# Splitting a unit's top-16 search and numbering between batches of dot products

## What is computed

```python
def peer(h, w_query, sub_keys, u_table, v_table):
    q = (x @ w_query).reshape(-1, PEER_HEADS, 2, KEY_DIM)
    s = jnp.einsum('nhid,hikd->nhik', q, sub_keys)
    top_s, top_i = lax.top_k(s, PEER_TOPK)
    cand_s = (top_s[..., 0, :, None] + top_s[..., 1, None, :])
    cand_i = (top_i[..., 0, :, None] * N_KEYS + top_i[..., 1, None, :])
    best_s, pos = lax.top_k(cand_s, PEER_TOPK)
    idx = jnp.take_along_axis(cand_i, pos, axis=-1)
    g = jax.nn.softmax(best_s, axis=-1)
    act = gelu(einsum('nd,nhkd->nhk', x, u_table[idx])) * g
    return einsum('nhk,nhkd->nd', act, v_table[idx])
```

## Time and profile before

| | before |
|---|---|
| median of 3 runs | 1032.12 us (1031.52 to 1033.51) |
| profiled execution | 1032.95 us, its span 1031.1 us |
| PE busy | 822.1 us (80%) |
| DVE busy | 669.9 us (65%) |
| ACT busy | 245.9 us (24%) |
| POOL busy | 420.1 us (41%) |
| gathers (queue q0) | 36864 packets, 268.45 MB |

### The profile page before, as it was taken

How to read it: one execution, slowest core, us unless ns; L and a number is a source line. 1 busy time by engine, 2 the same in 40 slices (tenths; PEclk the granted TensorE clock), 3 DMA queues, 4 the chain that set the end, 5 groups by cost and what they waited for, 6 DMA issues and landing times. The chain is left out here.

```text
span 1031.1 us, 9412 instructions
## 1 busy us (share of the span) xinstructions
PE 822.1 (80%) x2733; PEld 412.4 (40%) x2733; DVE 669.9 (65%) x1409; ACT 245.9 (24%) x764; POOL 420.1 (41%) x379
## 2 busy tenths in 40 slices
PE   5799867799888988779768787876777886877875
PEld 1276523346448964323323333332333332333332
DVE  7669999971337753477478568569579559645443
ACT  1421102125211123122222223132222213122120
POOL 1026756730001116455544453544543553644430
PEclk9999989999899999898998998998988998998898
DMA  9911126445033728999999999999999999999991
GB/s 360 401 32 64 75 89 237 176 174 215 0 123 139 291 82 332 422 422 421 422 421 422 422 422 421 421 421 422 421 421 421 422 422 420 421 421 422 421 401 48
DMA packets 43782, 322.54 MB, mean 313 GB/s; under 512 B 5768, under 2 KB 6600, under 8 KB 7520
## 3 DMA queue, kind: packets, MB, share of 16 engines
q0 software_dynamic: 36864, 268.45, 62.8%
q1 hardware_dynamic: 6512, 53.47, 13.3%
q10 hardware_dynamic: 368, 0.18, 0.1%
HBM read 320.86 MB, written 1.23 MB: 312 GB/s over the span
## 5 line engine op out<-in xcount | busy, mean ns | idle before, releaser
L737 PE MATMUL psum<-ring,arena 128*128 128x512 f32 x672 | 329.6, 649 | 90.3 <-ACT arena L982 90.2
L1437 DVE CUSTOM_DVE_ANT_0 ring<-ring,h 128x1024 f32<-128x1024 f32 x168 | 202.7, 1225 | 161.6 <-DMA ring<-uv_table,arena 160.6
L1093 POOL DMA_INDIRECT ring<-uv_table,arena x168 | 201.5, 1199 | 252.6 <-PE psum L737 187.0
L737 PEld LDWEIGHTS psum<-ring,arena 128*128 128x128 f32 x672 | 136.6, 208 | 282.6 <-issue 172.3
L737 PE MATMUL psum<-arena 128*128 128x512 f32 x352 | 170.6, 641 | 47.0 <-ACT arena L982 45.1
L1437 DVE CUSTOM_DVE_ANT_0 arena<-arena,h 128x1024 f32<-128x1024 f32 x88 | 106.4, 1225 | 75.2 <-DMA arena<-uv_table,arena 74.7
L1093 POOL DMA_INDIRECT arena<-uv_table,arena x88 | 105.9, 1203 | 120.8 <-PE psum L737 92.1
L737 PEld LDWEIGHTS psum<-arena 128*128 128x128 f32 x352 | 70.7, 205 | 145.4 <-issue 85.5
L969 ACT ACTIVATE small<-small 128x4 f32<-128x4 f32 x64 | 13.1, 205 | 421.8 <-DVE small L1437 421.7
L982 ACT ACTIVATE arena<-ident,small 128x128 f32<-128x128 f32 x256 | 80.8, 386 | 0.0
L1056 POOL TENSOR_TENSOR arena<-arena 128x512 f32<-128x512 f32 x32 | 52.7, 1665 | 41.6 <-DVE arena L1263 41.6
(11 more groups left out here) (158 smaller groups left out, 735.5 us busy)
## 6 DMA issues: line engine op xcount, KB each, us to landing
ring<-w_mod SPq DMA_DIRECT2D x12, 2048.0 KB, 10.7
ring<-w_query SPq DMA_DIRECT2D x4, 2048.0 KB, 7.4
ring<-w_out SPq DMA_DIRECT2D x2, 2048.0 KB, 8.4
ring<-uv_table,arena POOLq DMA_INDIRECT x168, 18.0
ring<-w_in_u SPq DMA_DIRECT2D x1, 2048.0 KB, 19.0
ring<-w_in_q SPq DMA_DIRECT2D x1, 1536.0 KB, 19.0
arena<-uv_table,arena POOLq DMA_INDIRECT x88, 19.1
ring<-w_in_kv SPq DMA_DIRECT2D x1, 1152.0 KB, 17.9
```

The costliest lines, as they stand in the source:

```text
L737: mm = pe.matmul(bank(f"acc_{g}_{half}"), diag[:, slot, :], rows[slot][:, D + 512 * half:D + 512 * half + 512], start=first and k == 0, st ...
L1093: pool.indirect_dma_start(rows[row], None, uv_table, bass.IndirectOffsetOnAxis(ap=idx[:, pick:pick + 1], axis=0)).then_inc(row_landed[row] ...
L1437: dve.tensor_tensor_reduce(out=rows[slot][:, 0:D], in0=rows[slot][:, 0:D], in1=h[:, it // NB, :], scale=1.0, scalar=0.0, op0=ALU.mult, op1 ...
```

## The change

For units 1 to 7 the search and the numbering are each cut in two halves of one head, with a batch of dot products between the pieces. `find(u)` and `number(u)` have the default argument `heads=(0, 2)`, both heads in one piece. Unit 0 is left as it is.

```diff
             for u in range(1, UNITS):
                 it = 8 * (u - 1)
-                find(u)
+                find(u, (0, 1))
                 if u == 1:
                     normalise(0)
                 products(it)
+                find(u, (1, 2))
                 products(it + 1)
-                number(u)
+                number(u, (0, 1))
                 products(it + 2)
+                number(u, (1, 2))
                 products(it + 3)
                 normalise(u)
```

## The result

| | before | changed |
|---|---|---|
| median | 1032.26 us (4 runs) | 1041.88 us (4 runs, 1039.20 to 1042.47) |
| ratio | | 1.0087, 95% interval 1.0067 to 1.0107 |
| the same again, beside other runs of before | 1031.47 us | 1040.55 us, ratio 1.0082 (1.0063 to 1.0101) |
| profiled execution, its span | 1032.95, 1031.1 us | 1042.47, 1040.7 us |

The ratio and its interval are worked out from all runs, so it need not be the quotient of the two medians. The changed kernel is slower by 0.8 to 0.9%, some 9 us. The forecast was 0.6%, 6.4 us. The second measurement was made to see which of the two holds; 1038.5 us was expected if unit 1's term is all there is, and 1040 to 1042 us if the first measurement holds. It gave 1040.55 us.

The account below looks back on a forecast made before the run. The gather stage runs at the pace of the transfers, so a delayed start moves everything: 1032.95 + 5.3 (late gelu) + 1.05 (PE clock) = 1039.3 us, as a median 1038.5. Own range 1037 to 1040.5; 8 in 10 for 1035.5 to 1044.

Parts of the forecast that it names:

- unit 1's term: Unit 1's split search delays the issue of pick 10 by 5.3 us plus 1.05 us of PE clock, 6.35 us.
- The start of the stage: Chain from unit 1's search through four dots, weigh(0), the copy query(1, 2) and PE to pick 10: 6.35 us late.
- from scores to projections, over before: PE, idle 8.8 us, returns at 1.2 GHz and loses 1.05 us more than before; bounds 0 to 1.3.
- pick 10, over before: POOL issues pick 10 at 395.9 in place of 389.51, moving the end by the same 6.35 us.
- The table switch: ACT's table load behind unit 1's exponential, no longer covered by the dots: 1.29 us from its start to gelu.
- Units 2 to 7: Gelu and pick 44's issue 3.2 us late in unit 2, hidden by the transfers: 0 us, bound 0 to 1 for unit 2.
- The slack: How late the gap pick's issue may be without delaying landings: 3.2 to 4.3 us for pick 44 in unit 2.
- The forecast's sign: In unit 2, pick 44 still lands at 2.484 us a pick behind pick 11; later landings would refute the forecast.
- Rival (a): Gathers starve in every unit as well as starting late: median 1043.4 or 1044.5 us; chance 15%.
- (b): Stage start delayed less, ACT or PE's clock recovering part: half of 5.3 us, no clock loss, 1034.8 us; chance 7%.
- (c): Batch 0's dots, 2.3 us earlier, offset the rest if the table is loaded elsewhere: nothing seen, 1032 us; chance 5%.
- (d): Faster: two short gaps in POOL's issues at each search avoid a 5.9 us stage loss, alone 1026.2 us; chance 4%.

Follow-up runs that it names:

- the doubled search: Against the kernel before: units 2 to 7 in halves with their second head searched twice, unit 1 unchanged; 1066.50 us, ratio 1.0320.
- all exponentials late: Changed kernel with unit 1's exponential on ACT moved just ahead of weigh(2), and those of units 2 to 7 two batches later; 1029.16 us, ratio 0.9963.

## Why the prediction came out as it did

**The start of the stage: right in every step.** Counted from the start of the search, in us:

| step | forecast | measured |
|---|---|---|
| first head | 6.13 | 6.09 (348.08 to 354.17, the end of L1380) |
| fourth dot done | 13.6 | 13.69 |
| exponential of unit 1 | 19.7 | 19.83 |
| gelu of weigh(0) | 21.27 | 21.37 |
| scores(1, 2) | 24.2 | 24.36 |
| from scores to projections, over before | 1.05 | 1.08 |
| pick 10, over before | 6.35 | 6.48 |

Moving the exponential on ACT removed the whole of it and more, and editing unit 1 alone brought it back, so the cause of these 6.5 us is shown.

**The table switch.** The forecast took 1.29 us from the load's start to the gelu, and it was 1.29 us (368.16 to 369.45). The Trainium skill's 2.66 us for a switch ("ScalarE: Activation LUTs", "What ACT_TABLE_LOAD costs") would have put the gelu at 22.7 in the table above. The trace agrees with the 1283 ns that the page gives for the load itself, and not with its further 1380 ns: the gelu came at 21.37, and a switch taken away in unit 2 gave back 1.41 us.

**Units 2 to 7: right in the mechanism, a term short in size.** The forecast took 0 for them. In the changed kernel gelu in unit 2 came 476.33 - 457.91 = 18.42 us into the search, as forecast, and pick 44 was issued 24.47 us into it, 3.25 us later than before; 3.2 was forecast. The slack, measured at 3.2 us by the doubled search, was just used up. The forecast's sign was to be read at pick 44, but in the changed kernel its dot marks no landing, since DVE is still behind with its work there. I read it at pick 48, for whose landing DVE waits in both kernels. In the changed kernel it came at 500.38 and was due at 456.76 + 42.23 = 498.99, so it was 1.4 us late. In the second profile of the same kernel pick 44 was again issued 24.47 us into the search, and pick 48 came at 497.15, due at 454.86 + 42.23 = 497.09, so nothing was lost. Rival (a) is thus at its edge: it happens in one execution of a kernel and not in another. Nor does it add up: at dot 255 the two profiles have lost 7.0 and 6.9 us since pick 11. Rival (a)'s 3.5 to 6 us did not come.

What the term of 0 missed is 0.9 to 1.2 us, 622.03 and 622.39 against 621.15. This is one step more of about 1 us, and moving the exponentials out of the way or taking their table loads away did not give it back. It goes with one more packet on the instruction queue.

**The rest.** 6.5 and 1.2 us make 7.7; the intervals of the two measurements, 6.5 to 11 us, hold it. The profiled execution's further 1.8 us lie ahead of the search. In the other profiles the search starts between 345.48 and 350.86 us, in kernels whose program is the same up to there, so the single execution does not tell whether the change has a part in it. In the second measurement the medians are 9.1 us apart, so up to some 2 us are noise or stay unexplained.

**How good the forecast was.** Both medians, 1041.88 and 1040.55 us, lie above the 1037 to 1040.5 that the forecast gave for its own mechanism. They lie inside the wider 1035.5 to 1044, whose upper part had been added for rival (a), and (a) is not what filled it. The start of the stage was foreseen for the right reasons. That the wider range held the rest is partly luck.

**The other rivals.** (b), a smaller delay, and (c), none, fell with the rows above. (d) saw a real loss: 5.9 us over the stage. It isn't the single long gap in POOL's issues. With all exponentials late, picks 43 and 44 are issued 5.7 us apart in place of 10.6, and the stage still loses 7.2 us between picks 11 and 255.

## What to carry to other kernels

Before a piece of work is split and something is put between the parts, look at which signal stands at the end of the last part, and what is queued behind the wait for it on every other engine. Here the gain on one queue was a loss on another, and moving the waiting instruction further down its queue turned 0.9% slower into 0.3% faster. In a stage at the pace of its transfers, count how late an issue may be. What lay within that cost nothing that could be measured here, and the start of the stage was what gave time back. The best version did without the halved search: it put the first batch of dots ahead of the search that had held it up.

## What the runs showed that I had not expected

The pace of landings breaks by about 1 us in six to eight steps behind pick 11, though the bytes moved in before show no dip. One of them in the kernel before, on DVE, picks 233 and 234, 3.43 us apart in place of 2.48:

```profile
955.09 1.23 DVE L1437 CUSTOM_DVE_ANT_0 ring<-ring,h 128x1024 f32<-128x1024 f32 x1 [1.26 <-DMA ring<-uv_table,arena]
958.52 1.28 DVE L1437 CUSTOM_DVE_ANT_0 ring<-ring,h 128x1024 f32<-128x1024 f32 x1 [2.19 <-DMA ring<-uv_table,arena]
```

The stage's length goes with the packets of the instruction queue: in the thirteen profiles without the doubled search it is 620.8 to 621.2 us with 23 of them and 621.7 to 622.5 with 24 or 25. The start of every packet is in the traces too, and it ties the two together. In these thirteen profiles there are 35 places where two dots in a row waited for their landings and the second came more than 0.5 us over the pace. Ahead of each of the 35 a packet of 8192 bytes started on q14, 1.8 to 3.0 us before the dot: at 956.4 us for the pair shown, and in the changed kernel at 610.9, 666.8, 743.8 and 985.8 us for dots at 613.0, 668.6, 746.5 and 987.9. A stage has only 16 or 17 such packets, some 38 us apart, so this is hardly chance. But most of them are followed by no break that can be seen, and what tells the one kind from the other stays open. That loads of instructions hold up the landings is the likeliest reading, by this tie in time and by the one experiment that added a load. By what means they do it is not shown, nor that it moves the median.

At the end of before the bytes drop to 49 GB/s at 1005 us, while the last row lands only at 1010.66. The DMA share there is 0.12. If two of the sixteen engines are busy and the others are not, that is 2/16, and these two lag some 5.6 us behind; this is an estimate, for the row doesn't say which engines they are.

```profile
1005.00:1006.00 1.00, 1.00 (x4) 0.43 (x3) 0.26 (x1) 0.00 (x0) 0.00 (x0) 1.00 0.12 49
```

In the changed kernel the drop comes only 3 us ahead of the last dot, which is at 1020.18:

```profile
1017.00:1018.00 1.00, 1.00 (x3) 0.38 (x2) 0.25 (x1) 0.00 (x0) 0.00 (x0) 1.00 0.26 107
```

This would explain how the bytes can dip in the changed kernel without a later landing: the engines that are ahead run dry first and lose their lead, and those that lag set the pace. That last step is argued, not shown.
